# Three seven-product pairs in a row in the FFN's first GEMM, with operands made beside the pair before

## The reference, cut to what matters

```
u = causal_dwconv(hn @ w_up, conv_w, conv_b)      # w_up 1024 x 5632, 3 taps
gate, val = u[..., :2816], u[..., 2816:]
return (silu(gate) * val) @ w_down
```

## Time and profile before

| | before |
|---|---|
| median of 3 runs | 2525.3 us (2525.03 to 2526.2) |
| profiled execution | 2525.95 us, span 2524.2 us |
| TensorE busy | 2470.5 us, 98% |
| VectorE busy | 1615.6 us, 64% |
| ScalarE busy | 1155.4 us, 46% |
| GpSimd busy | 602.3 us, 24% |

### The profile page before, as it was taken

How to read it: one execution, slowest core, us unless ns; L and a number is a source line. 1 busy time by engine, 2 the same in 40 slices (tenths; PEclk the granted TensorE clock), 3 DMA queues, 4 the chain that set the end, 5 groups by cost and what they waited for, 6 DMA issues and landing times.

```text
span 2524.2 us, 45974 instructions
## 1 busy us (share of the span) xinstructions
PE 2470.5 (98%) x18254; PEld 1724.5 (68%) x18254; DVE 1615.6 (64%) x2424; ACT 1155.4 (46%) x2166; POOL 602.3 (24%) x417
## 2 busy tenths in 40 slices
PE   8999999999999999999999999899999999999998
PEld 5566666666665667777766666676656777777665
DVE  6676777787868887777511276594379777772123
ACT  5455655666415554444311255595355444441111
POOL 1002113122142122232122113264411223221221
PEclk9999999999999999999999999999999999999999
DMA  3132222323132111212311112100121121213111
GB/s 118 54 104 79 85 84 80 97 68 99 45 127 101 51 51 50 65 35 66 126 46 58 40 34 68 34 2 18 43 110 50 51 66 34 66 56 126 46 57 67
DMA packets 67808, 167.69 MB, mean 66 GB/s; under 512 B 5680, under 2 KB 37840, under 8 KB 67408
## 3 DMA queue, kind: packets, MB, share of 16 engines
q1 hardware_dynamic: 67664, 165.70, 19.8%
HBM read 151.76 MB, written 12.86 MB: 65 GB/s over the span
## 4 chain that ended last, share of the span: by engine, by line
PE 86%; DVE 8%; ACT 3%; ACTq 1%; POOL 1%; issue 1%; DVEq 1%; DMA 0%
PE PS L2260 22%; PE PS L2262 22%; PE PS L2261 22%; PE PS L2661 4%; PE PS L2659 4%; PE PS L2660 4%; PE PS L2536 1%; PE PS L2543 1%; DVE BIG L1629 1%; PE PS L2525 1%; DVE TT L1693 1%; POOL BIG L869 1%; PE PS L2354 1%; ACT BIG L1539 1%; DVE R L460 1%
## 5 line engine op out<-in xcount | busy, mean ns | idle before, releaser
L2260 PE MATMUL PS<-R,whi 128*128 128x384 f16 (+2 forms) x2400 | 747.4, 311 | 2.6 <-DVE wlo L1594 1.6
L2262 PE MATMUL PS<-R,wlo 128*128 128x384 f16 (+2 forms) x2400 | 747.2, 311 | 0.0
L2261 PE MATMUL PS<-R,whi 128*128 128x384 f16 (+2 forms) x2400 | 747.1, 311 | 0.0
L1594 DVE SCALAR_TENSOR_TENSOR wlo<-stage,whi 128x1024 f16<-128x1024 f32 (+1 forms) x148 | 204.5, 1383 | 380.7 <-ACT whi L884 379.9
L2260 PE MATMUL PS<-BIG,whi 128*128 128x384 f16 (+2 forms) x1404 | 435.4, 310 | 4.9 <-DVE wlo L1594 4.2
L2262 PE MATMUL PS<-BIG,wlo 128*128 128x384 f16 (+2 forms) x1404 | 435.4, 310 | 0.0
L2261 PE MATMUL PS<-BIG,whi 128*128 128x384 f16 (+2 forms) x1404 | 435.3, 310 | 0.0
L2260 PEld LDWEIGHTS PS<-R,whi 128*128 128x128 f16 x2400 | 235.3, 98 | 127.7 <-issue 14.2
L2261 PEld LDWEIGHTS PS<-R,whi 128*128 128x128 f16 x2400 | 235.4, 98 | 121.3 <-issue 9.8
L2262 PEld LDWEIGHTS PS<-R,wlo 128*128 128x128 f16 x2400 | 235.4, 98 | 118.0 <-issue 1.0
L884 ACT ACTIVATE whi<-stage 128x1024 f16<-128x1024 f32 (+1 forms) x148 | 162.5, 1111 | 148.3 <-PE PS L2262 128.5
(11 more groups left out here) (285 smaller groups left out, 4556.7 us busy)
## 6 DMA issues: line engine op xcount, KB each, us to landing
stage<-wa SPq DMA_DIRECT2D x164, 512.0 KB, 3.5
stage<-wd SPq DMA_DIRECT2D x32, 704.0 KB, 4.0
TT<-cs_rows SPq DMA_DIRECT2D x32, 512.0 KB, 3.7
h_keep<-hT SPq DMA_DIRECT2D x2, 4160.0 KB, 12.4
EC<-cs_rows SPq DMA_DIRECT2D x64, 128.0 KB, 3.7
hT<-h SPq DMA_DIRECT2D x4, 1536.0 KB, 10.6
hT<-h_keep SPq DMA_DIRECT2D x4, 1536.0 KB, 8.5
out<-hT SPq DMA_DIRECT2D x4, 768.0 KB, 3.5
```

The source lines that it names most:

```text
L1594: eng.scalar_tensor_tensor(out=WL[d][:, 0:width], in0=stage[:, slot, 0:width], scalar=WS, in1=WH[d][:, 0:width], op0=ALU.mult, op1=ALU.sub ...
L2260: eng.matmul(acc, WH[slot][:, ws], xh, start=first, stop=False)
L2261: eng.matmul(acc, WH[slot][:, ws], xl, start=False, stop=False)
L2262: return eng.matmul(acc, WL[slot][:, ws], xh, start=False, stop=last)
```

## The change

The sequence of pairs from 7 on becomes 7 by seven products, 8 plain, 9 to 11 by seven, 12 plain, 13 to 15 by seven, 16 plain, 17 to 19 by seven, 20 plain, 21 by seven: 11 seven-product pairs and 4 plain ones in each layer. Inside a group of three the operands of the next pair are made during the pair ahead, each as soon as its own product there is done (`beside`). The order of the operands becomes that of the products. S2 gets a buffer of its own (`tmp2`, the other half of the same row), so three sums come first, then `hidden_lo`, then S4's. In the new `seven_pair` of TensorE the first six banks wait for VectorE's adds of the pair before. Only lines that differ in more than names are shown.

```diff
-NS = (KF - SF + 1) // 2
+RS = 3
+RP = RS + 1
+NR = (KF - SF - 3) // RP
+NS = 2 + RS * NR
-A11, A12, A22, S1, S3, S2, S4 = range(7)
+A11, S2, A12, S3, S1, A22, S4 = range(7)
+FIRST, REST = (A11, S2, A12, S3), (S1, A22, S4)
...
-        tmp = BIG[:, 21, 0:HP]
+        tmp, tmp2 = BIG[:, 21, 0:HP], BIG[:, 21, HP:2 * HP]
...
             def weight_sums(layer, m, i, n, before):      # GpSimd
                 if n > 0:
-                    eng.wait_ge(op_lo, m * 7 + (7 * (n - 1) + 6))
+                    eng.wait_ge(op_lo, m * (7 * RS) + 7 * n)
                 eng.tensor_tensor(tmp, a21, a22, ALU.add).then_inc(op_sum, 1)
                 eng.drain()
+                eng.tensor_tensor(tmp2, tmp, a11, ALU.subtract).then_inc(op_sum, 1)
                 eng.tensor_tensor(a21, a11, a21, ALU.subtract).then_inc(op_sum, 1)
+                eng.drain()
                 before()
-                eng.wait_ge(op_lo, m * 7 + (7 * n + 4))
-                eng.tensor_tensor(tmp, tmp, a11, ALU.subtract).then_inc(op_sum, 1)
-                eng.drain()
-                eng.tensor_tensor(a12, a12, tmp, ALU.subtract).then_inc(op_sum, 1)
+                eng.wait_ge(op_lo, m * (7 * RS) + (7 * n + A12 + 1))
+                eng.tensor_tensor(a12, a12, tmp2, ALU.subtract).then_inc(op_sum, 1)
...
             def op_high(layer, m, i, n, o, beside):       # ScalarE
+                if beside:
+                    eng.wait_ge(seven, m * (14 * RS) + (14 * (n - 1) + 2 * o + 2))
+                elif o == A11 and i > SF:
+                    eng.wait_ge(seven, m * (14 * RS) + 14 * n)
...
             def seven_pair(...):                          # ScalarE, behind the two copies
-                split_next(0)
-                split_next(1)
+                if split_next is not None:
+                    split_next(0)
+                    split_next(1)
+                if op_next is not None:
+                    for o in FIRST + REST[:-1]:
+                        op_next(o)
                 eng.drain()
...
                 up_tap(layer, m, i, 0)
+                if op_next is not None:
+                    op_next(S4)
...
-                with eng.Fori(0, NS - 1) as m:
-                    seven_pair(layer, m, 0, c0, gate, hidden, lambda s_: split(m * 2 + SF, s_))
-                    last_plain(m, 1)
+                seven_pair(layer, 0, SF, 0, c0, gate, hidden, lambda s_: split_plain(0, SF + 1, s_))
+                with eng.Fori(0, NR) as m:
+                    last_plain(m, SF + 1, 1)
+                    for j in range(RS - 1):
+                        seven_pair(layer, m, SF + 2 + j, 1 + j, c0, gate, hidden,
+                                   op_next=lambda o: op_high(layer, m, SF + 3 + j, 2 + j, o, True))
+                    seven_pair(layer, m, SF + RP, RS, c0, gate, hidden, lambda s_: split_plain(m, SF + RP + 1, s_))
+                last_plain(0, KF - 2, NS - 1)
...
             def seven_pair(...):                          # VectorE
                 for q in range(2):
                     add(4, q, c11[q], c11[q])
-                lo_next(0)
+                ops(A11, S2)                              # lo_next(0) where a plain pair follows
                 for q in range(2):
                     add(6, q, u3[q], u2[q])
-                lo_next(1)
+                ops(A12, S3)                              # lo_next(1) where a plain pair follows
                 for q in range(2):
                     add(8, q, u4[q], u2[q])
+                ops(S1)
                 eng.drain()
                 for q in range(2):
                     add(10, q, c21[q], u3[q])
                     eng.drain()
                     add(8, q, c22[q], u3[q])
+                ops(A22)
                 add(12, 0, c12[0], u4[0])
                 up_taps(layer, m, i, n0, 0, (1,))
                 add(12, 1, c12[1], u4[1])
                 up_taps(layer, m, i, n0, 0, (0,))
+                ops(S4)
                 up_taps(layer, m, i, n0, 1, (1, 0))
...
             def seven_pair(layer, m, i, n, behind_seven=False):   # TensorE
+                def free(bank):
+                    if behind_seven:
+                        eng.wait_ge(seven_v, m * (14 * RS) + (14 * (n - 1) + (6, 10, 12, 12, 12, 13)[bank]))
+                    else:
+                        eng.wait_ge(evac, m * (6 * RP) + (kept + bank + 1))
```

More of the change, by code:

```diff
@@ L792, in hidden_lo, with weight_sums @@
                                   ALU.subtract).then_inc(hid_lo, 1)
-            def weight_sums(layer, m, i0, before):
-                n = NS * layer + i0
+            def weight_sums(layer, m, i, n, before):
+                n += NS * layer
                 a11, a12, a21, a22 = stage[:, 1, 0:HP], stage[:, 1, HP:2 * HP], stage[:, 0, 0:HP], stage[:, 0, HP:2 * HP]
@@ L1459, in ffn_up, with last_plain @@
                     pair(i, KD * P, lambda: token_hi(layer, i - 2))
[L1461 to L1476, removed]
-                    seven_pair(layer, m, 0, c0, gate, hidden, lambda s_: split(m * 2 + SF, s_))
-                    last_plain(m, 1)
-                seven_pair(layer, 0, NS - 1, c0, gate, hidden, lambda s_: hi(U_DN[layer] + s_, KU * P))
+                def last_plain(m, i, n):
+                    i_ = m * RP + i
+                    for o in FIRST:
+                        op_high(layer, m, i + 1, n, o, False)
+                    take(i_, 0, i_)
+                    first_tap(i_, 0, UB[:, 0, :])
+                    for o in REST:
+                        op_high(layer, m, i + 1, n, o, False)
+                    gate(i_)
+                    take(i_, 1, i_)
+                    first_tap(i_, 1, UB[:, 1, :])
+                    hidden(i_)
+                last_plain(0, SF - 1, 0)
+                seven_pair(layer, 0, SF, 0, c0, gate, hidden, lambda s_: split_plain(0, SF + 1, s_))
+                with eng.Fori(0, NR) as m:
+                    last_plain(m, SF + 1, 1)
[4 more added lines that the diff above has]
+                last_plain(0, KF - 2, NS - 1)
+                seven_pair(layer, 0, KF - 1, NS - 1, c0, gate, hidden, lambda s_: hi(U_DN[layer] + s_, KU * P))
             ffn_up(0, lambda head: boundary(0, 1, J_OB, mix_r1, U_UP[0], head))
@@ L2055, in add, with ops @@
                                              op0=ALU.mult, op1=ALU.add).then_inc(seven_v, 1)
+                def ops(*os):
+                    if op_next is not None:
+                        for o in os:
+                            op_next(o)
                 c11, c12 = ([up_out(layer, 1, q, r) for q in range(2)] for r in (False, True))
@@ L2131, in ffn_up, with last_plain, lo_plain @@
                     pair(2 + kk, kk)
-                def last_plain(m, i0):
-                    i = m * 2 + (SF - 1 + 2 * i0)
+                def last_plain(m, i, n, plain):
+                    i_ = m * RP + i
                     for s_ in range(2):
[L2137 to L2146, removed]
+                        for o in (FIRST, REST)[s_]:
+                            op_low(layer, m, n, o)
+                        conv_tile(i_, s_, UB[:, s_, :], m * 2 + 2 * plain)
+                    product(i_)
+                def lo_plain(m, i):
+                    return lambda s_: split_lo(m * (2 * RP) + (u0 + 2 * i + s_ + 1), s_)
+                last_plain(0, SF - 1, 0, SF - 1)
+                seven_pair(layer, 0, SF, 0, product, lo_plain(0, SF + 1))
+                with eng.Fori(0, NR) as m:
+                    last_plain(m, SF + 1, 1, SF)
+                    for j in range(RS - 1):
+                        seven_pair(layer, m, SF + 2 + j, 1 + j, product, op_next=lambda o: op_low(layer, m, 2 + j, o))
+                    seven_pair(layer, m, SF + RP, RS, product, lo_plain(m, SF + RP + 1))
+                last_plain(0, KF - 2, NS - 1, KF - NS - 1)
+                seven_pair(layer, 0, KF - 1, NS - 1, product, lambda s_: lo(U_DN[layer] + s_, KU * P))
             def down(u0):
```

135 lines of the change are left out of this document (74 added, 61 removed).

## The result

The changed kernel takes 2558.68 us (median of 4 runs, 2557.37 to 2559.78); the kernel before took 2525.75 us in the same series. The ratio is 1.013, 95% interval 1.0113 to 1.0148: 33 us slower, where 2556.6 us had been forecast. The profiled execution took 2558.06 us around a span of 2555.9.

A forecast was written before the change was run, and what follows sets the result against it. TensorE bounds the kernel now; in the new groups VectorE's round, with ScalarE's copy behind it, would stall TensorE. 2525.95 - 15.1 saved + 39.4 stalls + 7 clock, less 0.65, gave 2556.6 us; range 2522 to 2567.

The forecast's parts named there:

- What is removed: In both layers, three plain pairs each become seven-product pairs: 15.1 us less TensorE work.
- What TensorE waits for: In a seven-product pair, the fourth product's second half waits for ScalarE's copy of product one; slack 1.3 us behind a plain pair.
- VectorE's round: First add to first add behind a seven-product pair making operands: 19.9 us without GpSimd, against TensorE's 18.62.
- the ladder: Step-by-step times through one group of three: copy late by 0.3, then stalls of 1.4 and 4.4 us; 39.4 over all groups.
- GpSimd's part: GpSimd's operations and VectorE's with two SBUF inputs exclude each other; one round's operands finish 3.4 us later than alone.
- The clock: TensorE's clock falls to half rate behind long waits, 2.4 us lost each; three of six charged, 7 us.
- Rival 1: TensorE's clock falls in every group: 14.4 us instead of 7, total 2564 us; chance 0.15.
- Sum: Whole kernel: 2525.95 - 15.1 + 39.4 + 7, less 0.65, gives 2556.6 us.
- Rival 2: GpSimd's sums fall into VectorE's idle times: stalls only 2.1 to 3.5 us a group, 2523 to 2531 us; chance 0.17.
- rival 3: VectorE's round fits TensorE's 18.62 us, so TensorE stays full and the whole saving shows: 2510 us; chance 0.08.
- rival 4: Second pair's operands come late, stopping TensorE at A11 or S2: 3 us a group gives 2570 or more; chance 0.05.
- The lower bound of the stalls: With no exclusion between GpSimd and VectorE, a group's stalls cost 0.7 + 1.4 = 2.1 us, 12.6 in all.

The follow-up runs named there:

- e1: The changed kernel with groups of one, so seven-product and plain pairs alternate as before: 2525.12 us, ratio 0.9998 to the kernel before.
- e3: The changed kernel, groups of three, with ScalarE's copy of product one moved ahead of `hidden` of the pair before: 2537.77 us, ratio 1.0049.
- e4: The changed kernel with groups of two and ScalarE's copy of product one ahead of `hidden` of the pair before: 2524.37 us, ratio 0.9997.
- e5: The changed kernel with extra unread matmuls ahead of TensorE's wait for ScalarE's copy, in each group's second and third pair: 2552.9 us, ratio 1.0104.
- e6: The changed kernel with GpSimd's sums for S3 and S4 made on 16 of 512 columns, part of the work omitted: 2545.22 us, ratio 1.0073.
- e7: The changed kernel with VectorE's first value-tile tap cut to 16 columns in pairs that make operands: 2547.78 us, ratio 1.008.
- e2: The changed kernel with groups of two seven-product pairs instead of three: 2545.73 us, ratio 1.0081 to the kernel before.

## Why the prediction was right, point by point

- *What is removed.* 15.1 us; the seven-product and plain pairs keep 18.62 and 21.16 us (the windows above; e1's timeline has the same steps). Right.
- *What TensorE waits for.* The second piece of the fourth product, released by the copy: each of the waits in the region. Right, and by e3 and e4 the copy's place alone costs 21 us.
- *VectorE's round.* 19.9 without GpSimd, 20 and 22 to 23 foreseen; 20.29 and 22.95 measured in the first group. The second rounds bear it out (22.14 to 23.38). The first rounds of layer 1 don't: they take 21.45, as VectorE starts 1.1 us earlier there and its first low half takes 2.24 us and not 0.96, which the ladder doesn't have. As the two cancel, the stalls hardly show it. Stalls of the first group: 0.3, 1.4, 4.4 foreseen; 0.41, 1.51, 4.03 measured. For the later groups of layer 0 the ladder had 0, 2.1, 4.4; they show 0.19, 1.50, 3.70 and about 0, 2.39, 3.48. Layer 1's last waits are shorter (3.2, 2.1, 1.9), and the clock fell there in the second pair already. With the waits filled (e5) they are some 3.5 long, so this is what shortened the last two, as the text allowed; the first, 3.2, it explains only in part.
- *GpSimd's part.* 3.4 us in the second round foreseen. The five low halves above take 1.38 + 1.53 + 2.58 + 1.08 = 6.57 against 0.68 + 0.68 + 1.28 + 0.68 = 3.32, 3.25 us more; e6 removes 1.9 of them with two of the four sums. Right.
- *The clock.* Charged with 7 us, as three falls of 2.4; 7.4 by e5. But it fell in five of six groups, seven times, so the size is right by luck: TensorE lost 12 us at the low level, and about 5 of them lay inside waits that were there anyway. Rival 1, by which the clock falls in every group and costs 14.4 us, was nearly right in how often and wrong in the price.
- *Sum.* 39.4 + 7 = 46.4 us was foreseen over the groups' matmuls, 46.4 measured; of these e5 puts 39.0 down to VectorE's round. An agreement to 0.1 us is luck too: the single groups lie between 5.9 and 9.2 us, around a mean of 7.7.
- Rival 2 (GpSimd falls into idle times) and rival 3 (the round fits) are refuted by the round's length, rival 4 (operands late) by the absence of any wait of TensorE on an operand. The lower bound of the stalls, 0.7 + 1.4 us a group with no exclusion, doesn't follow from the prediction's own figures: a round of 19.9 and a slack of 1.3 give none and about 1.2. Only the low end of rival 2 rests on it.

Outside the region the kernels differ by a few us from run to run: the clock's low stretches between 1260 and 1980 us cost 7 us in the profile before and 10 to 12 in three others (an estimate: half of TensorE's busy time in them). Differences of 0.1% therefore tell nothing here.

## What to carry to other kernels

When a stage that is bound by TensorE alternates with one that gives the other engines room, work out each engine's round for two such stages in a row before putting them so: a mean busy share of 64% hid rounds of 20.29 and 22.95 us against 18.62, that is 109% and 123%. Look at what stands in the queue ahead of the instruction that releases TensorE: moving one copy ahead of an unrelated cast was worth 21 us, and one of VectorE's low halves, moved into a wait, another 10. Shorten the round first and then choose how many fit: three in a row lost, two in a row with the round mended won 0.3%.

## What the runs showed of the hardware

- Beside GpSimd's operations, VectorE's low halves, with both inputs in SBUF, ran in turn with them, and a waiting operation got its turn between two of the other engine's: a low half ends at 1009.44, the GpSimd sum that started at 1008.85 at 1010.57, the next low half, begun at 1009.59, at 1011.12. Adds with an input in PSUM kept their 0.75 us for two.
- VectorE work that is saved can so turn into waiting: in e7 1.07 us less work shortened the first round by 1.0 us and the second by none.
- TensorE idle for 4.0 us had its clock at the 1.2 GHz level for the next 5 us; idle for 1.51 us it kept 2.4 GHz (first group). The wait's length alone does not tell: one of 3.70 us in the second group of layer 0 left PEclk at 1.00. Waits of 2.45 and 2.46 us in layer 1 were each followed by the low level, one of 2.39 in layer 0 was not; in e2 one of 2.24 us was, one of 2.45 was not.
- Filling such waits with matmuls that nobody reads (e5) kept the clock at 1.00 in the groups and made them 7.4 us shorter, the kernel 5.8 by the medians.
